# Routed experts: scatters of a block without waits between them, bias rows loaded a stage ahead, first weights behind a gather

## What is computed

```
x = x + merged @ w_out
h2 = rms_norm(x, ffn_norm_w)
logits = h2 @ w_router + b_router                  # 32 experts
top_vals, top_idx = top_k(logits, 4); gate = softmax(top_vals)
# tokens sorted by expert: 8192 (token, expert) pairs
hid = ragged_dot(xs, w_up, group_sizes) + b_up[e]  # 1024 -> 2048
act = glu * sigmoid(1.702 * glu) * (lin + 1)       # glu, lin clipped at 7
out = (ragged_dot(act, w_down, group_sizes) + b_down[e]) * gate   # 1024 -> 1024
y = zeros.at[tok].add(out);  x = x + y
```

## Time and profile before

| | us |
|---|---|
| median of 3 runs | 4795.08 |
| lowest, highest | 4794.27, 4798.69 |
| span of the profiled execution | 4794.9 |
| PE busy | 4611.9 (96%) |
| DVE busy | 2994.2 (62%) |
| ACT busy | 2193.5 (46%) |
| POOL busy | 430.6 (9%) |

### The profile page before, as it was taken

How to read it: one execution, slowest core, us unless ns; L and a number is a source line. 1 busy time by engine, 2 the same in 40 slices (tenths; PEclk the granted TensorE clock), 3 DMA queues, 4 the chain that set the end, 5 groups by cost and what they waited for, 6 DMA issues and landing times.

```text
span 4794.9 us, 95932 instructions
## 1 busy us (share of the span) xinstructions
PE 4611.9 (96%) x29214; PEld 4230.1 (88%) x29215; DVE 2994.2 (62%) x5644; ACT 2193.5 (46%) x4080; POOL 430.6 (9%) x423
## 2 busy tenths in 40 slices
PE   6999999999899799999699999999999999999997
PEld 5888888888577678788699999999999999999997
DVE  7655565555588744355677777767665666565654
ACT  5222222222477622122466666666555555555553
POOL 0000000000233100022101001101101010101000
PEclk8999999999899999999799999999999999999998
DMA  5332343222444433454577677767676666666654
GB/s 193 110 119 99 125 155 111 103 103 100 166 161 161 183 129 134 146 166 135 156 226 216 208 225 225 211 193 218 185 217 192 205 201 195 192 200 183 196 164 115
DMA packets 573960, 806.07 MB, mean 168 GB/s; under 512 B 51217, under 2 KB 516625, under 8 KB 566801
## 3 DMA queue, kind: packets, MB, share of 16 engines
q1 hardware_dynamic: 548032, 718.01, 45.5%
q0 software_dynamic: 25808, 86.59, 7.5%
HBM read 650.25 MB, written 154.21 MB: 168 GB/s over the span
## 4 chain that ended last, share of the span: by engine, by line
PE 50%; DMA 1%; SPq 0%; issue 0%; ACT 0%; DVE 0%; POOLq 0%; ACTq 0%; DVEq 0%; POOL 0%
PE e_acc L2677 11%; PE e_acc L2679 11%; PE e_acc L2678 11%; PE e_acc L2671 8%; PE e_acc L2672 4%; PE e_xT L2636 1%; PE e_yp L2645 1%; PE e_acc L2675 1%; DMA e_raw<-in_w_up 1%; PE e_acc L2674 1%; DMA out<-e_ys,e_rec_out 0%; SPq L2314 0%; DVE e_x_both L2533 0%; ACT e_whi L2412 0%; ACT e_ys L2454 0%
## 5 line engine op out<-in xcount | busy, mean ns | idle before, releaser
L2527 DVE TENSOR_TENSOR e_wlo<-e_raw,e_whi 128x512 fp32r<-128x512 f32 x1552 | 1054.3, 687 | 495.6 <-ACT e_whi L2412 465.3
L2412 ACT CAST e_whi<-e_raw 128x512 fp32r<-128x512 f32 x1552 | 959.0, 647 | 163.8 <-DMA e_raw<-in_w_up 130.2
L631 PE MATMUL p_acc<-p_hi,a_hi 128*128 128x464 f32 x1792 | 670.0, 374 | 10.2 <-DVE p_lo L521 10.2
L633 PE MATMUL p_acc<-p_hi,a_lo 128*128 128x464 f32 x1792 | 668.9, 373 | 0.0
L632 PE MATMUL p_acc<-p_lo,a_hi 128*128 128x464 f32 x1792 | 666.6, 372 | 0.0
L2677 PE MATMUL e_acc<-e_x_both,e_whi 128*128 128x272 f32 (+3 forms) x2176 | 648.0, 298 | 2.8 <-DVE e_lin L2558 2.8
L2679 PE MATMUL e_acc<-e_x_both,e_whi 128*128 128x272 f32 (+3 forms) x2176 | 645.0, 296 | 0.0
L2678 PE MATMUL e_acc<-e_x_both,e_wlo 128*128 128x272 f32 (+3 forms) x2176 | 644.9, 296 | 0.0
L2677 PE MATMUL e_acc<-e_ahi,e_whi 128*128 128x272 f32 (+6 forms) x2048 | 598.9, 292 | 0.0
L2679 PE MATMUL e_acc<-e_alo,e_whi 128*128 128x272 f32 (+6 forms) x2048 | 588.3, 287 | 0.0
L2678 PE MATMUL e_acc<-e_ahi,e_wlo 128*128 128x272 f32 (+6 forms) x2048 | 588.1, 287 | 0.0
(11 more groups left out here) (349 smaller groups left out, 7762.9 us busy)
## 6 DMA issues: line engine op xcount, KB each, us to landing
e_raw<-in_w_up SPq DMA_DIRECT2D x1040, 256.0 KB
e_raw<-in_w_down SPq DMA_DIRECT2D x512, 256.0 KB
p_raw<-in_w_in SPq DMA_DIRECT2D x64, 928.0 KB, 4.8
z<-p_z SPq DMA_DIRECT2D x32, 928.0 KB, 4.0
z<-p_u SPq DMA_DIRECT2D x32, 928.0 KB, 3.9
b_gates<-z SPq DMA_DIRECT2D x16, 1536.0 KB
oT<-x_oT SPq DMA_DIRECT2D x16, 1024.0 KB, 9.6
b_raw<-oT SPq DMA_DIRECT2D x16, 1024.0 KB
```

Of the source, the lines that this page charges most:

```text
L631: pe.matmul(out, a_hi[:, j, at], hi[:, k, :], start=k == 0, stop=False)
L633: mm = pe.matmul(out, a_lo[:, j, at], hi[:, k, :], start=False, stop=k == HALF_K - 1)
L2412: act.copy(held(w_hi, u), loaded(u)).then_inc(hi_made.sem, 1)
L2527: dve.tensor_tensor(held(w_lo, u), loaded(u), held(w_hi, u).bitcast(F32), ALU.subtract).then_inc(lo_made.sem, 1)
```

## The change

Five edits. (1) `scatter` waits for the scatters of the blocks before its own, no longer for the earlier tiles of its own block. (2) The four loads of bias rows are issued by SP in `finish_mixing`, behind the last load of x, into a fixed place at the end of SBUF. (3) In `run_experts` SP issues four units of the first block, waits until the first gather has landed, and then issues the other twelve. (4) In `finish_mixing` PE turns h2 of tile 15 before the prefix of tile 14. (5) The bias rows have no place of their own in `run_experts` any more, so its other tensors lie 3 KB lower.

```diff
+class BiasRows:
...
+    def load(self, sp, io):
+        for i in range(self.ROWS):
+            es = slice(i * E // self.ROWS, (i + 1) * E // self.ROWS)
+            sp.dma_start(self.up[i][:], io["b_up"][es, :].rearrange("e (c n) -> (e c) n", c=self.CHUNKS)).then_inc(
+                self.loaded.sem, 16)
+            sp.dma_start(self.down[i][:], io["b_down"][es, :].rearrange("e (c n) -> (e c) n", c=self.CHUNKS)).then_inc(
+                self.loaded.sem, 16)
...
             load_x(TILES - 1, 1)
+            bias_rows.load(sp, io)
 
             store(TILES - 2, 0)
             store(TILES - 1, 1)
...
+            turn_h2(TILES - 1, 1)
             prefix(TILES - 2)
-            turn_h2(TILES - 1, 1)
             score(TILES - 1)
...
             load_records(1)
-            for i in range(BIAS_ROWS):
...
-            e = Block(sp, 1).get(EXPERT, E - 1)
-            for u in range(HELD):
+            first = Block(sp, 1)
+            e = first.get(EXPERT, E - 1)
+            for u in range(PARTS):
+                load(0, u, e)
+
+            sp.wait_ge(x_in.sem, (first.prior + first.live) * 16)
+            for u in range(PARTS, HELD):
                 load(0, u, e)
...
                     pool.wait_ge(y_gated.sem, block.out(1, i) + 2)
-                    pool.wait_ge(y_sent.sem, (block.prior + i) * 16)
+                    pool.wait_ge(y_sent.sem, block.prior * 16)
                     pool.wait_ge(rec_moved.sem, block.row)
```

More of the change, by code:

```diff
@@ L1473, in source, with __init__ @@
         return io[name][(k - first) * P:(k - first + 1) * P, :]
+class BiasRows:
+    CHUNKS = FF // P
+    ROWS = E * CHUNKS // P
+    def __init__(self, nc, sems):
+        bottom = SBUF_END - self.ROWS * 3 * P * 4
+        self.bottom = bottom
+        self.up = [nc.alloc_sbuf_tensor_at(f"e_bup{i}", [P, 2 * P], F32, offset=bottom + 3 * i * P * 4)
+                   for i in range(self.ROWS)]
+        self.down = [nc.alloc_sbuf_tensor_at(f"e_bdown{i}", [P, P], F32, offset=bottom + (3 * i + 2) * P * 4)
+                     for i in range(self.ROWS)]
+        self.loaded = Signal(sems, nc, "e_bias_in", 16)
+    def load(self, sp, io):
[5 more added lines that the diff above has]
+                self.loaded.sem, 16)
 class OutWeights(Weights):
@@ L1701, in entry, with finish_mixing @@
     return ds(column * (ROWS + 1) + row, 1)
-def finish_mixing(nc, io, ident, blocks, weights):
+def finish_mixing(nc, io, ident, blocks, weights, bias_rows):
     H = 512
@@ L2182, in _, with run_experts @@
             mm.then_inc(ordered.sem, 1)
-def run_experts(nc, io, ident, blocks):
+def run_experts(nc, io, ident, blocks, bias_rows):
     PAIR = 2 * P
@@ L2203, in run_experts @@
         w_hi, w_lo = sb("whi", [P, HELD, KU, PAIR], F32R), sb("wlo", [P, HELD, KU, PAIR], F32R)
-        up_rows = [sb(f"bup{i}", [P, 2 * P]) for i in range(BIAS_ROWS)]
-        down_rows = [sb(f"bdown{i}", [P, P]) for i in range(BIAS_ROWS)]
+        up_rows, down_rows, bias_in = bias_rows.up, bias_rows.down, bias_rows.loaded
         bias = sb("bias", [P, E, 3 * CHUNKS])
@@ L2218, in run_experts @@
         rec_in, rec_now, rec_out = (sb(f"rec_{n}", [P, BLOCK_TILES, 2], I32) for n in ("in", "now", "out"))
+        assert nc.sbuf_base <= bias_rows.bottom
         acc = [c.enter_context(nc.psum_tensor(f"e_acc{i}", [P, 512], F32)) for i in range(4)]
@@ L2228, in run_experts @@
         rec_loaded, rec_kept, rec_moved, idle = sig("rec_loaded", 16), sig("rec_kept"), sig("rec_moved"), sig("idle")
-        bias_in, bias_turned, bias_made = sig("bias_in", 16), sig("bias_turned"), sig("bias_made")
+        bias_turned, bias_made = sig("bias_turned"), sig("bias_made")
         up_kept, down_kept, yT_cleared, rec_cleared = sig("up_kept"), sig("down_kept"), sig("yT_cleared"), sig("rec_cleared")
@@ L2783, in build @@
             blocks = s.enter_context(nc.sbuf_tensor("blocks", [1, COLS * (ROWS + 1)], I32))
-            finish_mixing(nc, io, ident, blocks, out)
+            bias_sems = []
+            bias_rows = BiasRows(nc, bias_sems)
+            finish_mixing(nc, io, ident, blocks, out, bias_rows)
             sems.extend(out_sems)
             end_stage(nc, sems)
-            run_experts(nc, io, ident, blocks)
+            sems.extend(bias_sems)
+            run_experts(nc, io, ident, blocks, bias_rows)
 _INS = ["x", "mem", "mix_norm_w", "mem_norm_w", "w_in", "swa_q_norm_w", "swa_k_norm_w", "swa_sinks", "ret_norm_w",
```

## The result

The changed kernel takes 4839.74 us (median of four runs, 4829.14 to 4849.07) against 4796.89 before: ratio 1.0092, 95% interval 1.0080 to 1.0104. It is slower by 43 us where 17 were forecast, and outside the stated range of 4781 to 4830. The profiled execution has a span of 4846.8 us, 51.9 more than before; it is one of the two slowest of the four. A few executions further down were slow throughout (6600 us and more); they are left out of every ratio and move the medians by 0.2 us at most, but for one kernel, whose median is given without them. I read the profile in the order of the prediction, ends first.

The account below looks back on a forecast made before the run. PE was taken to bound the expert stage, working almost without a break. Gains 2.7 + 1.3 + 8.3 = 12.3 off a span of 4794.9 give 4782.6; plus 29 lost in the stage, 4811.6, so 4812; range 4781 to 4830.

Parts of the forecast that it names:

- The turn of tile 15: End of the routing stage: PE's turn of tile 15 starts 2.75 us earlier, ahead of the prefix; gain 2.7, bounds 2.0 and 2.8.
- The start of the expert stage: First weights issued some 2.0 us earlier, twelve units no longer competing with the gather; gain 1.3, from 0.5 lost to 2.5.
- The end: Last block's three scatters issued without waits between them land sooner; gain 8.3 us, bounds 5.4 and 9.2.
- What the edit does inside the stage: Three-tile blocks 272 or 288 wide: back-to-back scatters delay weights, PE waits; 12 x 2.4 = 29 us lost, bounds 0 and 44.
- R+20.9: Fifth weight unit's expected split, in us after the block's records are copied (R), if behind gathers and scatter 1; 3.7 late.
- the second case: Per-block PE wait of 3.7 us with the fifth unit late, against 1.1 when the sixth unit is late.
- R+17.2: Latest time the fifth unit may come without PE waiting, in us after the block's records are copied (R).
- Span and median: Whole kernel: the timed median was taken to lie 0.2 us above the profiled span.
- the weights hold: Expert stage: the three scatters move without PE noticing; 4783, between 4780 and 4788; chance 0.28.
- Only the sixth unit is late: Expert stage: scatter 1's data keep their place; 13 lost, 12.3 won, 4796, between 4790 and 4802; chance 0.20.
- The edit does nothing at the end: Last block: one queue's DMAs move one after another anyhow; end wins 5.4 only, adding 3 us; no chance of its own.
- The bound of 44 for the stage: Upper bound of the loss inside the expert stage: 12 blocks x 3.7 us of PE waiting.

## Why the prediction was wrong

The direction and the mechanism were right: the fifth unit of weights falls behind the scatters, and PE waits. What failed is the term for it, 12 x 2.4 = 29 us, against 61.6 us measured in the profile. Step by step:

- *The turn of tile 15*: forecast 2.7. Alone it gave 2.7 by the medians, with an interval that includes no change; in the profiles the turn starts 0.06 us after h2 instead of 2.8. Right.
- *The start of the expert stage*: forecast 1.3 on top, measured nothing that can be told from zero. The weights did come 3.7 us earlier, but the gather, then moving beside them, took 1.2 us longer. I had let the weights be last by 0.7 us; now the gather is.
- *The end*: forecast 8.3, measured 8.1 in the profile after and 7.7 with this edit alone, 6.7 by its medians. Right, and so is the reason: the three scatters' data need 8.95 us of all engines, where 3 x 2.9 was reckoned. The step of 0.8 for branches was 0.3.
- *What the edit does inside the stage*: this is the term that failed. The fifth unit was forecast at about R+20.9, and came at R+20.3 to 21.7 in twelve of the fifteen. The waits of the 272 and 288 wide blocks were forecast at 29 us and grew by 28.5. That they meet is luck: 2.4 was the mean of two cases, 1.1 and 3.7, and in nine of these twelve blocks the fifth unit came as late as in the second case; two blocks in which POOL was late, one in between, and a later deadline in the 288 wide blocks (fifth unit at R+20.4, wait 2.45: about R+18) brought the sum down again. For the 272 wide ones R+17.2 was right (R+20.3, wait 3.17).
- *What the term left out*: first, a wait of PE was priced at its length alone. Products at 1.2 GHz behind the longer waits cost 21.5 us more, and no term stood for them, though the window of the earlier trace rows shows the granted clock at 0.50 where PE stands. Second, "the wider blocks have longer pairs and PE never waits in them" was read from blocks in which the fifth unit comes at R+15.5. It now comes 5 us later, and 304 wide blocks wait 1.5 to 2.5 us each, 5.6 in all. Third, the stretch with two scatters to a block, priced at nothing, lost 6.0, of which 4.2 are waits of PE. Over all profiles this stretch loses 4.0 to 8.1 in the five in which a whole scatter 1 follows the gathers without a pause, and 1.2 or less in the six changed kernels in which it waits; by what path such an early scatter 1 makes PE wait there was not traced. So 28.5 + 21.5 + 5.6 + 6.0 = 61.6 against 29, and 9.8 won against 12.3 (2.0 at the start, 7.8 from the copy of the last block's records to the end): 52 in the profile, 43 in the median.
- *Span and median*: the 0.2 us added at the end compares two executions. Of one and the same execution the time is 1.7 us above the span (4848.49 and 4846.8). That PE waits for nothing else in the stage was short by 0.8 us, in the first block.
- *Rivals*: "the weights hold" fell with the scatter edit alone. "Only the sixth unit is late" describes the kernel in which only scatter 2 is free: there it is true, and no change is what it gives (ratio 1.0004). "The edit does nothing at the end" fell: with this edit alone the end is 7.7 us shorter.

The bound of 44 for the stage was built from one kind of block and one kind of cost; with the 21.5 us for the clock on top, the range would have reached past 4840.

## What to carry to other kernels

A wait between two transfers can be what lets a third one through: before taking it away, see who shares the engines with it, and how long the packets of its queue are against the other's. Price a new wait of PE with the slow products behind it: here 21.5 us on top of 34 in one execution, 11.5 on top of 20 in another. And a wait that is worth dropping at the end, where nobody else uses the engines, is not for that reason worth dropping in the loop: make it a parameter (4784 us against 4838).

## What the hardware showed

- Weights beside scatters, both queues busy: packet for packet. With scatter packets of 4 KB the weights get 45 to 47 GB/s, with 2 KB 80 to 89.
- Losses don't add up: 13 and 8 us for either wait, 43 for both.
- From the issue of the second gather to PE's turn of its first tile: 7.7 to 8.5 us in the six profiles in which the first weights are issued ahead of it, 6.9 to 7.6 in the seven in which they are issued after it.
- A wait of 4.2 us was followed by 6 us at a granted clock of 0.50. With ten products ahead of the wait, what the clock held back over the fifteen blocks fell from 20.5 us to 1.7.
